# A sample unit of 80 columns, with its pooling moved from TensorE to VectorE, in a hybrid decoder step

## The reference, cut to what matters

```python
def _pool_mix(u, buf, start_pos, w_group, scale):      # buf: the 15 rows before u
    ext = jnp.concatenate([buf, u], axis=1)
    c = jnp.pad(jnp.cumsum(ext, axis=1), ((0, 0), (1, 0), (0, 0)))
    for gi, w in enumerate((2, 4, 8, 16)):             # 4 groups of 128 channels
        hi, lo = c[:, 16:16 + T, sl], c[:, 16 - w:16 - w + T, sl]
        outs.append((hi - lo) / minimum(w, pos + 1) - u[:, :, sl])
    mixed = einsum('btgc,gcd->btgd', stack(outs), w_group)
    return mixed * scale, ext[:, -15:]

h = RMSNorm(x);  u, q, k, v, og, zr, ga, gb = split(h @ w_in)
A = pool_mix(u) @ w_pool_proj;  B = GLA(q, k, v, gate(zr), state) gated by og @ w_gla_proj
x = x + (sigmoid(ga) * A + sigmoid(gb) * B) @ w_out
x = x + SwiGLU(RMSNorm(x));  y = RMSNorm(x)
```

## Time and profile before

| | |
|---|---|
| median of 3 runs | 930.46 us (929.46 to 930.49) |
| the profiled execution | 929.21 us, span of its slowest core (core 3) 928.0 us |
| spans of the 8 cores | 922.9 to 928.0 us |
| TensorE busy | 889.3 us, 96% |
| VectorE, ScalarE, GpSimd busy | 442.0, 257.2, 111.2 us |
| DMA | 101.29 MB moved, 109 GB/s over the span |

### The profile page before, as it was taken

One profiled execution on the slowest core, in us unless ns is written; L12 is line 12 of the kernel. 1 busy time (PEld: TensorE's weight loads), 2 busy tenths in 40 slices (PEclk: granted clock), 3 DMA queues, 4 the chain that ended last, 5 costly groups with the idle time before them and its releaser, 6 DMA issues.

```text
span 928.0 us, 14428 instructions; the slowest of 8 cores (922.9 to 928.0 us)
## 1 busy us (share of the span) xinstructions
PE 889.3 (96%) x4864; PEld 454.8 (49%) x4864; DVE 442.0 (48%) x725; ACT 257.2 (28%) x504; POOL 111.2 (12%) x217
## 2 busy tenths in 40 slices
PE   0998999999999999999999999999999999999996
PEld 0544456665555466546654444444444444444442
DVE  3576655656633522342246665656562331242236
ACT  1635153322322212202224442332231101101122
POOL 6300011201200000100112100120120000000002
PEclk9999999999999999999999999999999999999999
DMA  8964574456773956463876897336575662372503
GB/s 176 238 127 82 78 108 69 65 108 120 136 112 60 182 112 97 87 136 69 124 103 182 174 239 122 46 54 85 89 128 97 98 118 39 59 131 46 91 24 159
DMA packets 57657, 101.29 MB, mean 109 GB/s; under 512 B 42089, under 2 KB 42618, under 8 KB 50274
## 3 DMA queue, kind: packets, MB, share of 16 engines
q0 software_dynamic: 10560, 67.55, 43.6%
q1 hardware_dynamic: 46576, 32.68, 14.5%
q10 hardware_dynamic: 450, 0.15, 0.3%
HBM read 140.57 MB, written 11.40 MB: 164 GB/s over the span
## 4 chain that ended last, share of the span: by engine, by line
PE 92%; DMA 4%; issue 1%; DVE 1%; ACT 1%; POOL 0%; DVEq 0%; ACTq 0%; POOLq 0%
PE ps L447 87%; DMA xres<-xp 2%; DMA ring<-w_f 1%; DMA ring<-w_a 1%; PE ps L551 1%; DVE R L344 1%; PE ps L755 1%; ACT R L338 0%; PE ps L736 0%; PE ps L432 0%; PE ps L719 0%; PE ps L756 0%; PE ps L1004 0%; PE ps L635 0%; POOL xres L205 0%
## 5 line engine op out<-in xcount | busy, mean ns | idle before, releaser
L447 PE MATMUL ps<-hT,ring 128*128 128x512 bf16 (+3 forms) x2728 | 512.4, 345 | 1.7 <-DMA ring<-w_f 1.0
L447 PEld LDWEIGHTS ps<-hT,ring 128*128 128x128 bf16 x2728 | 262.1, 98 | 233.1 <-issue 6.0
L338 ACT ACTIVATE sgt<-ps 128x512 f32<-128x512 f32 (+3 forms) x217 | 115.1, 532 | 447.2 <-PE ps L447 391.3
L447 PE MATMUL ps<-ring,R 128*128 128x512 bf16 (+1 forms) x1020 | 222.5, 379 | 0.0
L344 DVE TENSOR_TENSOR R<-ps,sgt 128x384 bf16<-128x384 f32 (+2 forms) x110 | 66.5, 605 | 239.0 <-PE ps L447 231.6
L447 PEld LDWEIGHTS ps<-ring,R 128*128 128x128 bf16 (+1 forms) x1020 | 100.8, 99 | 118.6 <-issue 1.2
L344 DVE TENSOR_TENSOR xres<-xres,ps 128x512 f32<-128x512 f32 (+1 forms) x102 | 69.7, 686 | 66.2 <-PE ps L447 65.9
L340 ACT ACTIVATE R<-xres 128x1024 bf16<-128x1024 f32 (+2 forms) x44 | 45.6, 1037 | 99.4 <-DVE xres L348 43.4
L447 PE MATMUL ps<-R,ring 128*128 128x384 bf16 (+2 forms) x320 | 71.0, 344 | 0.0
L447 PE MATMUL ps<-ring,hT 128*128 128x512 bf16 (+1 forms) x280 | 66.0, 391 | 4.7 <-ACT hT L338 4.7
L205 POOL DMA_DIRECT2D ring<-w_f x34 | 18.7, 550 | 293.9 <-PE ps L447 292.6
(11 more groups left out here) (102 smaller groups left out, 433.1 us busy)
## 6 DMA issues: line engine op xcount, KB each, us to landing
ring<-w_f POOLq DMA_DIRECT2D x30, 1024.0 KB, 12.1
ring<-w_a POOLq DMA_DIRECT2D x24, 1024.0 KB, 11.9
...
```

Source lines behind the costliest of these rows:

```text
L338: T.op('act', lambda e: e.activation(out=out, in_=in_, func=func, scale=scale, bias=bias), reads=rd, writes=wr)
L447: return [(lambda e, k=k: e.matmul(out, lhsT=lw(k), rhs=rx(k), start=(k == 0), stop=(k == K - 1))) for k in range(K)]
```

## The change

The unit `S` becomes 64 sample tokens and then 16 meta tokens, without padding (`SR` = 80, `NS` = 64), and is loaded by one DMA from one tensor. MC is 1104, and `X`, `Y`, `Z` are 368 columns each. The sample tokens' pooling is done feature-major on VectorE: `u` of block `S` is copied into four tiles `xe` of 16 sequences x 19 columns that already hold the 15 columns of history, and `swindows` adds windows there. The meta tokens' 16 columns stand in `Eb` ahead of the prompt (offset 15 to 30), `windows('A', g)` of pass 0 runs over 543 columns, and two more instructions of 16 columns turn its first part into the meta tokens' result. The state of the meta tokens is formed over 80 rows with the key rows of the samples set to zero.

```diff
-SR = 96
+SR = 80
+NS = 64
-    BLK = {'S': (SC, SR), 'A': (0, 512), 'B': (512, 512), 'X': (0, 384), 'Y': (384, 384), 'Z': (768, MC - 768)}
+    BLK = {'S': (SC, SR), 'A': (0, 512), 'B': (512, 512), 'X': (0, 368), 'Y': (368, 368), 'Z': (736, 368)}
-            T.dma(q, 'd_x8', [(xres[0:16, 8, :], meta[:, :]), (xres[32:96, 8, :], xs[:, :])], writes=[xres[0:96, 8, :]])
+            T.dma(q, 'd_x8', [(xres[0:SR, 8, :], xm[:, :])], writes=[xres[0:SR, 8, :]])
-    mset(xres[0:32, 8, :], 0.0)
-    T.dma('pool', 'd_hi', [(hist[0:120, 0, :], spool[0:120, :]), (hist[0:120, 1, :], spool[120:240, :])], writes=[hist])
-    T.dma('pool', 'd_ws', [(gffn_bc[:, 0:864], wsd[:, 0:864]), (ws3[:, :], wsd[:, 864:1152])],
-          writes=[gffn_bc[:, 0:864], ws3[:, :]])
+    T.dma('pool', 'd_hi', [(gfin_bc[:, 0:608], hist[:, 0, :]), (gffn_bc[:, 0:608], hist[:, 1, :])],
+          writes=[gfin_bc[:, 0:608], gffn_bc[:, 0:608]])
+    mset(Eb[:, :, 0:15], 0.0)
...
+    xe = [(gfin_bc if g < 2 else gffn_bc)[:, (g % 2) * 304:(g % 2 + 1) * 304].rearrange("p (s t) -> p s t", s=16) for g in range(4)]
...
+        def wsums(E, n, g):
+            ln = n - 1
+            a = wtmp[0][:, 0:ln]
+            tt(a, E[:, 1:n], E[:, 0:ln], ALU.add)
+            bi, sh = 0, 2
             for lv in range(g):
                 ln -= sh
                 tt(wtmp[1 - bi][:, 0:ln], wtmp[bi][:, sh:sh + ln], wtmp[bi][:, 0:ln], ALU.add)
...
+            return wtmp[bi][:, 0:ln]
+
+        def windows(blk, g):
+            w = 2 << g
+            m = 16 if (blk == 'A' and p == 0) else 0
+            e0 = 16 - m if blk == 'A' else 528
+            n = 15 + m + 512
+            E = Eb[:, g, e0:e0 + n]
+            ws = wsums(E, n, g)
+            o = 16 - w
             c0 = BLK[blk][0]
+            stt(pooled[:, g, c0:c0 + 512], ws[:, o + m:o + m + 512], 1.0 / w, E[:, 15 + m:527 + m], ALU.mult, ALU.subtract)
+            if m:
+                mt = ws[:, o:o + 16]
+                tt(mt, mt, cs[:, C_RC + 16 * g:C_RC + 16 * g + 16], ALU.mult)
+                tt(pooled[:, g, SC + NS:SC + SR], mt, E[:, 15:31], ALU.subtract)
+
+        def swindows(g):
+            w = 2 << g
+            lo, ln = 16 - w, w + 2
+            ta = [x[:, 0:288].rearrange("p (s t) -> p s t", s=16) for x in wtmp]
+            E = xe[g]
+            tt(ta[0][:, :, 0:ln], E[:, :, lo + 1:lo + 1 + ln], E[:, :, lo:lo + ln], ALU.add)
+            bi, sh = 0, 2
+            for lv in range(g):
+                ln -= sh
+                tt(ta[1 - bi][:, :, 0:ln], ta[bi][:, :, sh:sh + ln], ta[bi][:, :, 0:ln], ALU.add)
...
+            stt(pooled[:, g, SC:SC + NS].rearrange("p (s t) -> p s t", s=16), ta[bi][:, :, 0:4], 1.0 / w, E[:, :, 15:19],
+                ALU.mult, ALU.subtract)
...
             if blk == 'S':
-                act(Eb[:, g, 0:15], ps[:, 1:16], AF.Copy)
+                act(Eb[:, g, 15:31], ps[:, NS:SR], AF.Copy)
+                act(xe[g][:, :, 15:19], ps[:, 0:NS].rearrange("p (s t) -> p s t", s=16), AF.Copy)
                 return
...
-        def upool_s1(rg):
-        def upool_s2(g):
...
-                kr = 16 if isS else 128
+                kr = SR if isS else 128
+                if isS:
+                    kl = kdm[0][0:SR, 0, :]
+                    sg_ = cs[0:SR, C_SEG + 16:C_SEG + 17]
+                    T.op('dve', lambda e: e.tensor_scalar(out=kl, in0=kt[0:SR, :], scalar1=sg_, scalar2=None, op0=ALU.mult),
...
-            T.dma('sp', 'd_pbh', [(pbh[:, :, :], spool.rearrange("(s r) c -> s r c", r=15)[:, 4:15, :])])
...
-            upool_s1(ru)
             slab_release(j_u)
+            T.dma('sp', 'd_pbs', [(pbs[:, 0, :], gfin_bc[:, 0:608]), (pbs[:, 1, :], gffn_bc[:, 0:608])],
+                  reads=[gfin_bc[:, 0:608], gffn_bc[:, 0:608]])
...
-            og_all(rog, [lambda: upool_s2(0), lambda: (upool_s2(1), windows('B', 2)), lambda: upool_s2(2),
-                         lambda: (upool_s2(3), windows('B', 3))])
+            og_all(rog, [lambda: windows('B', 2), lambda: windows('B', 3), lambda: swindows(0), lambda: swindows(1),
+                         lambda: swindows(2), lambda: swindows(3)])
```

More of the change, by code:

```diff
@@ L28 @@
 C_MAS = 256
[L29 to L32, removed]
+C_SEG = 336
+C_D0 = 354
+C_D0S = 866
+C_RC = 946
+NCS = 1010
 def _build_consts():
@@ L41, in _build_consts @@
     seg = np.full(128, -1)
[L42 to L45, removed]
+    seg[0:NS] = np.arange(NS) // 4
+    seg[NS:SR] = 16
     same = (seg[:, None] == seg[None, :]) & (seg[:, None] >= 0)
-    c[:, C_MAS:C_MAS + 96] = (same & (j <= i))[:, :96]
-    for s in range(16):
-        c[32 + 4 * s:36 + 4 * s, C_SEG + s] = 1.0
+    c[:, C_MAS:C_MAS + SR] = (same & (j <= i))[:, :SR]
+    for s in range(17):
+        c[:, C_SEG + s] = (seg == s)
     d0 = np.ones(512, np.float32)
@@ L52, in _build_consts @@
     c[:, C_D0:C_D0 + 512] = d0
[L53 to L58, removed]
-    for g, w in enumerate((2, 4, 8, 16)):
[L60 to L83, removed]
+    d0s = np.ones(SR, np.float32)
+    d0s[0:NS:4] = 0.0
+    d0s[NS] = 0.0
+    c[:, C_D0S:C_D0S + SR] = d0s
+    for g, w in enumerate((2, 4, 8, 16)):
+        c[:, C_RC + 16 * g:C_RC + 16 * g + 16] = 1.0 / np.minimum(w, np.arange(16) + 1)
+    return c
 class Trk:
@@ L235, in build_program @@
     w_f2 = din("w_f2", [2, 128, 3072])
-    cst = din("consts", [128, NCS]); wsd = din("wsd", [128, 1152])
+    cst = din("consts", [128, NCS])
     y_p = dout("y_p", [2048, D]); y_s = dout("y_s", [64, D]); pbp = dout("pbp", [128, 4, 15])
-    gsp = dout("gsp", [128, 2, 128]); pbu = dout("pbu", [64, 512]); pbh = dout("pbh", [16, 11, 512])
+    gsp = dout("gsp", [128, 2, 128]); pbs = dout("pbs", [128, 2, 608])
     gss = dout("gss", [128, 16, 2, 128])
@@ L287, in build_program @@
     keT = bfv(R1, 0, 2 * MC).rearrange("p (a n) -> p a n", a=2)
-    wtmp = [f32v(R1, i * 2112, 528) for i in range(2)]
+    wtmp = [f32v(R1, i * 2176, 544) for i in range(2)]
     cumb = [f32v(R1, 12672, 1024), f32v(R2, 12288, 1024)]
-    Eb = f32v(R2, 0, 4 * 1039).rearrange("p (g n) -> p g n", g=4)
+    Eb = f32v(R2, 0, 4 * 1055).rearrange("p (g n) -> p g n", g=4)
     merged = bfv(R2, 0, 8 * MC).rearrange("p (a n) -> p a n", a=8)
@@ L570, in decs @@
                 if blk == 'S':
-                    cpy(decS[:, :, 0:16], eT[:, :, 35:96:4])
-                    cpy(decS[:, :, 16:17], eT[:, :, 15:16])
+                    cpy(decS[:, :, 0:16], eT[:, :, 3:NS:4])
+                    cpy(decS[:, :, 16:17], eT[:, :, SR - 1:SR])
                 else:
@@ L612, in ogproj @@
             tt(G2[0:r, us, :].rearrange("p (h v) -> p h v", h=4), sg.rearrange("p (h v) -> p h v", h=4), g4, ALU.mult)
-        def windows(blk, g):
-            w = 2 << g
-            e0 = 0 if blk == 'A' else 512
-            E = Eb[:, g, e0:e0 + 527]
-            tt(wtmp[0][:, 0:526], E[:, 1:527], E[:, 0:526], ALU.add)
-            off, ln, sh = 14, 526, 2
-            bi = 0
+        def wsums(E, n, g):
[3 more added lines that the diff above has]
+            bi, sh = 0, 2
             for lv in range(g):
@@ L1216 @@
     shared = {
-        "meta": f(meta_tokens), "g_mix": f(g_mix).reshape(1, D), "g_ffn": f(g_ffn).reshape(1, D), "g_final": f(g_final).reshape(1, D),
+        "g_mix": f(g_mix).reshape(1, D), "g_ffn": f(g_ffn).reshape(1, D), "g_final": f(g_final).reshape(1, D),
         "g_gla_norm": f(g_gla_norm).reshape(1, 128),
@@ L1240 @@
     gla_p = np.stack([R[c]["gsp"].reshape(2, 64, 2, 128).transpose(2, 0, 1, 3).reshape(4, 64, 128) for c in range(8)], 0)[None]
-    pool_s = np.concatenate([np.concatenate([R[c]["pbh"], R[c]["pbu"].reshape(16, 4, 512)], 1) for c in range(8)], 0)[None]
+    pool_s = np.concatenate([R[c]["pbs"].reshape(128, 4, 16, 19)[:, :, :, 4:19].transpose(2, 3, 1, 0).reshape(16, 15, 512)
+                             for c in range(8)], 0)[None].astype(np.float32)
     gla_s = np.concatenate([R[c]["gss"].reshape(2, 64, 16, 2, 128).transpose(2, 3, 0, 1, 4).reshape(16, 4, 64, 128)
```

74 lines of the change are left out of this document (31 added, 43 removed).

## The result

The changed kernel takes 933.68 us (median of 6 runs, 932.97 to 935.16) against 929.69 us for the kernel before in the same session: ratio 1.0045, 95% interval 1.0033 to 1.0057. By the ratio that is 4.2 us slower (4.0 us between the medians); the forecast was 3.2 us slower, and 933.5 us.

What follows compares the result with a forecast made beforehand. TensorE, busy 96% of the span, was taken as the bound. The terms -2.1 + 12.5 + 0.2 - 3.8 - 3.6 gave +3.2 us, 933.7 us against the median, stated as 933.5, with a range of 930 to 937.

Steps and rivals of the forecast that it cites:

- The new wait: Stage 1: ScalarE's copy into xe waits for the history loads, TensorE stands 9.8 us, gk of S starts 12.5 us late.
- Start: First loads: POOL no longer waits for VectorE's clearing and issues one load less; everything up to stage 2 comes 2.1 us earlier.
- a first issue near 1.1 us: Sign that the forecast is right: POOL's first load issued near 1.1 us, against 2.90 us before.
- The pooling leaves TensorE: og and qk stretch up to sB1: TensorE loses S pooling, VectorE gains it, 3.8 us gained; second windows('A', 3) costs 0.2.
- The small steps: VectorE's 14 swindows instructions: 0.26 us each plus columns at 0.96 per ns, 5.1 us in all.
- Columns: Gates and feed-forward: 544 products per block at 0.416 ns per column, with 16 columns fewer, gain 3.6 us.
- The clock: TensorE resumes at 1.2 GHz after the long gap; without that fall gk would be 10.75 us late instead of 12.5.
- Rival 1: Both history loads land before 39.3 us, so ScalarE does not wait: 922.4 us, faster; chance 0.16.
- rival 2: Milder wait: history lands 1 us earlier and the clock does not fall on resuming: 930.9 us, no change; chance 0.19.
- Rival 3: VectorE's new work is hidden and TensorE sets the og and qk stretch: 929.8 us, no change; chance 0.06.
- Rival 4: Longer wait: history lands 3 us later and the clock falls a second time: 938 us, slower; chance 0.09.
- rival 5: Small VectorE instructions have a fixed part of 0.15 us, not 0.26: 2.0 us less, 931.7 us, no change; chance 0.03.

Runs made afterwards that it cites:

- e3: Kernel before plus one ScalarE copy of a single history element behind the first of the four copies at 39 us: 941.18 us, ratio 1.0126.
- e2: Changed kernel with the samples' u copied into free tile sqb first, then into the history tiles after block A's last u product: 922.74 us, ratio 0.9927.
- e6: Changed kernel with VectorE clearing 32 rows of unit S first, so POOL's first load waits again: 934.36 us, ratio 1.0051.
- e5: Changed kernel without the 14 swindows instructions, the samples' pooled columns cleared instead: 930.74 us, ratio 1.0011.
- e4: Changed kernel with column blocks of 384, 384 and 336 instead of three of 368: 932.86 us, ratio 1.0041.
- e11: Changed kernel with the scaled meta keys written by ScalarE straight from PSUM instead of by VectorE at the head of sB1: 931.03 us, ratio 1.0023.
- e1: Changed kernel with the two history loads issued ahead of weight slab 2 instead of behind it: 926.13 us, ratio 0.9962.
- e10: Changed kernel with samples' u through scratch, doubled A3 steps issued once, swindows moved into gate preparation, meta keys scaled by ScalarE: 917.27 us, ratio 0.9869.

## Why the prediction was right, step by step

**The new wait** (+12.5): right in place and mechanism, and with the start taken off nearly in size: +9.9 us at `gk` on the mean of the cores, forecast 10.4. Forecast were a ScalarE wait of 11 us and a TensorE gap of 9.8; they are 10.32 and 9.35. Alone, in e3, it costs 11.7 us (forecast 10.8 for that kernel, which lacks the meta instructions); taken away, in e2, the time falls by 10.9 us (forecast 11.3). The landing came at 47.6 us, forecast 50.4 - 2.1 = 48.3.

**Start** (-2.1): TensorE's first products start at 22.82 us on core 0, which stood at 24.80 before, 2.0 us earlier; on the mean of the cores it is 2.7 us, with 0.5 to 4.5 on single ones. The sign that I had named, a first issue near 1.1 us, did not come: it is at 1.59, 1.3 us earlier than before instead of 1.8, and 1.8 with the issue that is saved. The size of the term is not settled, by e6 either.

**The pooling leaves TensorE** (-3.8 + 0.2): this term was too large by 1 us. From `gk` to `sB1` cores 0 and 3 took 53.6 us before and take 51.0 and 49.4 after, -2.6 and -4.2; the six other cores took 51.9 and take 49.4 to 49.6, -2.4. The mean is -2.6, forecast -3.6. I had worked from core 3, and of the stretch at half clock at 80.6 to 84.0 us, which I took off there, only cores 0 and 3 show anything: the granted clock from 78 to 90 us is 0.86 on them and 1.00 on the six others. The wait of 1.75 us ahead of it, which I took off as well, occurs on cores 0, 3 and 6 alone; on the five others TensorE already runs at half clock behind `gk` of block `B`, comes later, and does not wait. VectorE is last, as its sum said: after `swindows` it works without a gap of over 0.2 us up to the scaling at 120.23 us. But TensorE is not far behind it: e5, without `swindows`, gains 1.4 us there and not the 3.9 us that were left up to the 7.7 us of TensorE alone. The small steps cost what the two rows gave, 0.17 us each and 2.0 us for `swindows(3)`. By the table of operation costs in "VectorE: DVE Perf Modes", section on the TRN2 errata (the Trainium skill), a 16-column one would take an estimated 0.08 us, and the section itself says that this row of the table comes out too short for a single operation; the trace has 0.17 and the measurement decides.

**Columns** (-3.6): right. From the first gate product to pass 1 the cores gain 3.6 us (377.35 to 373.75), and the price per product is right to 0.1 ns. By e4, 0.5 us of it are due to the even split. What is missing is a term that I left out, behind `sB1`: the f32 transposes of L769 take 1.97 us, 1.09 before on six of the eight cores, and the way from `sB1` to the gates is 0.4 us longer on the mean. All eight cores run them at half clock after the change, two of eight (cores 1 and 5, 1.96 and 1.90 us) before. I had priced the wait at `sB1`, not what the clock makes of that stretch. That the wait is the cause is not shown: e11 has no wait at `sB1`, and seven of its cores run the transposes at half clock, wholly or in part.

**The clock.** I gave it 1.75 us once, behind the long gap. The first products there took 3.57 us, so that was right, but the mean granted clock of the cores fell from about 0.995 to 0.987. Half-clock stretches also follow the gap of 2 us at `gk` of `S` (on core 0 alone) and the 0.82 us at `gk` of block `B` (on the seven others, on five cores before), and stand behind `sB1` (on all cores). "TensorE: Matmul & The Clock Gate", section on HAM oscillation (the Trainium skill), tells of a kernel whose clock is throttled anew at each wait for a load, and the waits that it names are longer than these; here gaps of 2.2 to 2.9 us, and shorter ones on some cores, were followed by half clock in e1, e2, e10 and the changed kernel.

**How much of it was luck.** The sum is 0.8 us under the mean of the cores. The terms are off by -0.5 (wait and start), +1.0 (pooling) and +0.4 us (behind `sB1`), so they cancel in part. The range of 930 to 937 us was meant for this: landing times differ by over 2 us from core to core, and only the slowest core is timed.

Rival 1 (922.4 us) came true as soon as its condition was made true: 922.7. Of rival 2, the earlier landing came in part (0.7 us on core 0), the clock fell all the same. Rival 3 fell, as TensorE waits 2.02 us for VectorE at `sB1`. Rival 4, a longer wait, and rival 5, cheaper small instructions, fell.
